# A mixture-of-experts stage on one core: expert weights split in halves ahead of their blocks, down projection in f16

## The chip, the core and the metric

The program runs on one core of one Trainium2 chip. Its time is the device time of one execution in microseconds (us). The core has TensorE (PE; its weight loads are listed apart as PEld), VectorE (DVE), ScalarE (ACT), GpSimd (POOL) and SyncE (SP), each with an instruction stream of its own; they meet at semaphores only. Transfers are issued from the queues of SP, ACT and POOL.

## What is computed

A block of an encoder on 4096 tokens of width 1024, in two stages. The mixer (norm, input projection, a linear recurrence beside a gated delta rule, output projection, residual) isn't changed in what it computes. Behind it each token goes to two of 32 experts, and each expert is a gated MLP with a hidden width of 256:

```
p_sel, g_sel = top_k(softmax(x @ group_w + group_b), 1)
top_logits, top_idx = top_k(expert logits of the chosen group, 2)
gates = p_sel * softmax(top_logits)
h = silu(xb @ w_gate[e]) * (xb @ w_up[e])      # 1024 -> 256
y = h @ w_down[e]                              # 256 -> 1024
out[token] += y * gate
```

A last norm follows. All inputs are f32. The 8192 assignments are sorted by expert; each expert's share is cut into blocks of 128 rows.

## The kernel before

**Mixer stage.** A software pipeline over 33 tiles of 128 tokens, written out by hand: `body(s)` of each engine names the parts of several tiles in one order. It takes 63 to 64 us a step and is followed by a table of the expert blocks (L1654 to L1684) that VectorE writes and TensorE turns into one row. Between other work, ScalarE also sums the squares of w_gate and w_up of one expert in each step from the fourth on (`raw_squares`, L917: eight chunks of 512 columns, squared in place in `ht`). SP loads the chunks into the two halves of `ht`, each when the square before the last is done (`raw_chunks`, L487). From the sums comes a scale for each expert, so that the weights fit f16. Step -1 has one expert to sum and step 0 has two; steps 1 and 2 have none.

**Expert stage.** `blocks` (L1810) runs 5 blocks written out, then pairs in a loop with a run-time limit, then two more. Each block knows its expert from a table `blk`. Four slots in `W` hold the raw f32 weights of four experts (1 MB each of gate, up and down); SP refills a slot when the last down product of its expert is done (L1854 to L1857), and says `w_ready` for the expert before. What one block asks of each engine, in program order:

- POOL gathers 128 rows of normed tokens (L1874), reads the next block's token numbers (L1866) and adds the output rows of three blocks earlier to `h_rows` in HBM (L1906).
- ScalarE makes the high f16 part of the next block's gate and up weights, eight instructions of 512 columns (`high_part`, L1982), each with a signal of its own; the sigmoid (L2002); the high part of the next rows (L1991); half of the previous block's output (L1968); the copy of the turned hidden rows, in f32 (L2009).
- VectorE makes the low part of the same weights, raw times scale minus high, eight instructions, each after its own high part (`low_part`, L2038); the hidden rows (L2061 and L2065, with the token's gate in the second); the low part of the next rows (L2022); the other half of the output (L2045); the column of scales for a later block (L2031).
- TensorE: gate/up in three f16 products (high x high, high x low, low x high; 24 matmuls of 512 columns, L1946), the turn of the next rows (L1920), the down product of the block before in f32 (four matmuls of 512 columns, shown as eight, L1930), the turn of the hidden rows (L1956).

The weights of an expert are thus split anew for each of its blocks, into two buffers `wx` in turn. A wait by VectorE in the low parts:

```
for k in range(KT):
    dve.wait_ge(sem("wx_high"), KT * b + k + 1)
    a = nc.vector.scalar_tensor_tensor(out=part_of(wx[par][:, 1], k), in0=raw[:, k], ...)
```

## Time and profile before

| | us |
|---|---|
| runs (three) | 3265.24, 3267.44 (median), 3268.61 |
| span of the profiled execution, first to last instruction | 3263.7 |
| PE busy | 2990.4 (92%) |
| DVE busy | 2590.6 (79%) |
| ACT busy | 1997.9 (61%) |
| POOL busy | 949.3 (29%) |

The time of the profiled execution itself isn't listed apart from these three; its span lies 3.7 us below their median, for what is around the first and last instruction. Busy time is time in which an engine executes; matmuls are pipelined, so that a duration of one is more than the distance to the next, and distances between starts are the ones to read. "[1.00 <-ACT W L1982]" behind a row means: the engine sat idle for 1.00 us until ScalarE's instruction of line 1982 on tile W was done; "issue" means that nothing the profile shows was waited for. The mixer stage fills the span up to about 2300 us, the expert stage up to about 3175, the last norm the rest. Mean granted TensorE clock: 0.968 of full speed.

### The profile page before, as it was taken

What the parts mean: (1) busy time and instruction counts of PE and PEld (TensorE: products, weight loads), DVE (VectorE), ACT (ScalarE), POOL (GpSimd) and SP (SyncE); (2) the same over time, 40 slices, a digit from 0 to 9 for tenths busy, and PEclk for the clock granted to TensorE, in tenths of its full rate; (3) what the DMA queues carried; (4) which work ended last, traced back from release to release, by engine and by line L of the source; (5) the groups of instructions that cost most, each with busy time, mean ns of one, the idle gap of its engine ahead of it and who ended that gap; (6) DMA issues with size and microseconds to landing.
All of it is one profiled execution on the core that took longest, in us unless ns stands there. A gap on an engine that the chain in (4) does not pass through costs nothing. (4 is left out here: it accounts for less than half of the span.)

```text
span 3263.7 us, 81939 instructions
## 1 busy us (share of the span) xinstructions
PE 2990.4 (92%) x28778; PEld 2233.3 (68%) x28779; DVE 2590.6 (79%) x7206; ACT 1997.9 (61%) x4412; POOL 949.3 (29%) x994
## 2 busy tenths in 40 slices
PE   3777999999999999999999999997699999999970
PEld 3766878888887888788878888885344555555430
DVE  6878778887887888788878887886788888888755
ACT  4555566666665656565666666653577777777646
POOL 4313122212221222132222212221344444544420
PEclk9889999999999999999999999998899999999985
DMA  7010111211212111212111111214387877677749
GB/s 264 27 53 14 47 66 65 67 66 66 72 63 76 60 67 66 73 60 73 66 66 65 68 66 66 72 56 200 118 255 222 243 202 214 187 219 216 220 99 394
DMA packets 117811, 380.30 MB, mean 117 GB/s; under 512 B 18560, under 2 KB 18688, under 8 KB 105216
## 3 DMA queue, kind: packets, MB, share of 16 engines
q1 hardware_dynamic: 82528, 269.96, 22.6%
q0 software_dynamic: 29216, 89.30, 11.9%
q10 hardware_dynamic: 5760, 16.85, 1.3%
q8 instruction: 204, 3.34, 0.4%
q14 instruction: 103, 0.84, 0.1%
HBM read 280.05 MB, written 96.01 MB: 115 GB/s over the span
## 5 line engine op out<-in xcount | busy, mean ns | idle before, releaser
L578 PE MATMUL pj<-uT,W 128*128 128x128 f16 x15840 | 982.9, 220 | 0.0
L578 PEld LDWEIGHTS pj<-uT,W 128*128 128x128 f16 x15840 | 936.8, 98 | 45.7 <-issue 37.6
L2038 DVE SCALAR_TENSOR_TENSOR W<-W,ecol 128x512 f16<-128x512 f16 x664 | 447.6, 747 | 111.9 <-ACT W L1982 107.4
L1982 ACT ACTIVATE W<-W,ecol 128x512 f16 x664 | 416.2, 710 | 79.7 <-issue 77.2
L1946 PE MATMUL bA<-W,uT 128*128 128x512 f16 x1992 | 446.6, 381 | 5.4 <-issue 4.1
L1946 PEld LDWEIGHTS bA<-W,uT 128*128 128x128 f16 x1992 | 193.5, 98 | 228.6 <-issue 9.1
L1741 POOL TENSOR_TENSOR dec<-tri,g 128x512 f32<-128x512 f32 x33 | 34.4, 1042 | 925.6 <-DVE g L1461 925.6
L1930 PE MATMUL pj<-W,qs 128*128 x664 | 301.8, 598 | 1.9 <-issue 1.0
L917 ACT ACTIVATE ht<-ht 128x512 f32<-128x512 f32 x256 | 159.9, 627 | 94.6 <-DMA ht<-w_up 90.2
L1930 PEld LDWEIGHTS pj<-W,qs 128*128 128x128 f32 x664 | 120.9, 192 | 123.3 <-issue 122.9
L947 ACT ACTIVATE qh<-bA 128x256 f32<-128x256 f32 x198 | 76.8, 388 | 193.4 <-PE bA L678 188.1
L638 PE MATMUL bO<-W,yl 128*128 128x512 f16 x768 | 186.4, 383 | 5.0 <-DVE yl L1375 5.0
L595 PE MATMUL pj<-W,uT 128*128 128x512 f16 x792 | 186.7, 379 | 0.5 <-POOL W L1692 0.5
L1777 POOL TENSOR_TENSOR yg<-aahh,gg 128x512 f32<-128x512 f32 x33 | 41.9, 1271 | 482.1 <-DVE yl L1375 457.8
L638 PE MATMUL bO<-W,yt 128*128 128x512 f16 x768 | 178.4, 378 | 0.0
L1155 DVE SCALAR_TENSOR_TENSOR qs<-ext_q,cvw,qs 128x128 f32<-128x128 f32 x396 | 168.2, 485 | 1.2
L678 PE MATMUL bA<-dec,Mt 128*128 128x128 f32 x792 | 134.2, 292 | 11.5 <-DVE dec L1303 11.1
L1906 POOL DMA_INDIRECT h_rows<-lath,sid x42 | 71.7, 1706 | 245.0 <-issue 121.1
L1906 POOL DMA_INDIRECT h_rows<-aahh,sid x41 | 71.0, 1731 | 203.6 <-issue 99.8
L595 PEld LDWEIGHTS pj<-W,uT 128*128 128x128 f16 x792 | 73.9, 98 | 71.7 <-issue 0.7
L1313 DVE COPY_PREDICATED X<-lvl,bB 128x256 f32<-128x256 uint8 x165 | 82.3, 499 | 50.5 <-PE bB L691 47.6
L691 PE MATMUL bB<-X,qh 128*128 128x128 f32 x660 | 113.4, 295 | 6.7 <-ACT qh L947 3.2
(444 smaller groups left out, 6310.0 us busy)
## 6 DMA issues: line engine op xcount, KB each, us to landing
ht<-w_gate SPq DMA_DIRECT2D x128, 256.0 KB, 3.2
ht<-w_up SPq DMA_DIRECT2D x128, 256.0 KB, 3.4
W<-w_gate SPq DMA_DIRECT2D x32, 1024.0 KB
W<-w_up SPq DMA_DIRECT2D x32, 1024.0 KB
W<-w_down SPq DMA_DIRECT2D x32, 1024.0 KB
x_in<-xm SPq DMA_DIRECT2D x33, 512.0 KB, 4.5
ht<-xm SPq DMA_DIRECT2D x32, 512.0 KB, 3.5
h_rows<-ht SPq DMA_DIRECT2D x32, 512.0 KB
```

The source lines that it names most:

```text
L578: mm = pe.matmul(pj[g % 2][:, j, :], w16[:, k, w_half(w_high, COL[GROUPS[g]], 512, j * P, P)], (ul if low_u else uh)[:, k, :], start=(k == ...
L595: mm = pe.matmul(flat(pj[1]), u[:, k, :], w16[:, k, w_half(w_high, c, 512)], start=(k == 0 and n_pass == 0), stop=(k == KT - 1 and n_pass ...
L638: mm = pe.matmul(bOf[:, 512 * half:512 * half + 512], y, wo16[:, j, w_half(w_high, 512 * half, 512)], start=(j == 0 and not w_high), stop= ...
L678: mm = pe.matmul(bA[:, q, :], Mt[:, 2 + q, :], crossed(T, b, P * q, HALF // b), start=True, stop=True)
L691: mm = pe.matmul(bB[:, q, :], Y[:, q, :], crossed(X, b, P * q, HALF // b), start=True, stop=True)
L917: nc.scalar.activation(ht[:, 512 * (c % 2):512 * (c % 2) + 512], ht[:, 512 * (c % 2):512 * (c % 2) + 512], ACT.Square, accum_out=sqc[:, n, ...
L1155: a = nc.vector.scalar_tensor_tensor(out=dst[:, j, :], in0=src, scalar=w, in1=dst[:, j, :], op0=ALU.mult, op1=ALU.add)
L1906: pool.indirect_dma_start(out=h_rows, out_offset=bass.IndirectOffsetOnAxis(ap=sid[par][:], axis=0), in_=yo[par], in_offset=None, compute_o ...
L1930: mm = pe.matmul(flat(pj[half]), hm2[:, j, :], w[:, j, 512 * half:512 * half + 512], start=(j == 0), stop=(j == 1))
L1946: mm = pe.matmul(flat(bA), x[:, k, :], wx[par][:, part, k, :], start=(k == 0 and part == 0 and x is uh), stop=(k == KT - 1 and x is ul))
L1982: nc.scalar.activation(part_of(wx[par][:, 0], k), raw[:, k], ACT.Copy, scale=ecol[par][:, k:k + 1]).then_inc(sem("wx_high"), 1)
L2038: a = nc.vector.scalar_tensor_tensor(out=part_of(wx[par][:, 1], k), in0=raw[:, k], scalar=ecol[par][:, k:k + 1], in1=part_of(wx[par][:, 0] ...
```

## The change

- **Splitting.** Each expert now has two halves (four of the eight gate/up pieces, and one of the two rows of w_down each). In every block ScalarE makes four high parts and VectorE four low ones of a half of the *next* expert, in a buffer per parity of the expert: block 0 of an expert the first half, every later block the second. VectorE waits once, for all four high parts. The first expert is split whole ahead of block 0. Each expert gets at least two blocks (`LEAST`), so that both halves are made.
- **Down projection.** w_down is split also, with a scale of its own (1024 columns in each half, one instruction on each engine). The hidden rows are divided by their largest absolute value, turned, and split into high and low f16; three f16 products take the place of the f32 one (12 matmuls of 512 columns). The row's scale and gate go into the evacuation, all of which is now ScalarE's.
- **Raw slots.** Three instead of four. SP refills a slot when its expert is split, and says `w_ready` for an expert in its next iteration.
- **Sums of squares.** Twelve chunks instead of eight for each expert in the mixer stage; the four of w_down are squared at other places of `body`.
- The table has more columns (expert ahead, addresses of raw and split weights), read by six small matmuls instead of three.

The diff, cut to its core:

```diff
-ZEROED = 16 * (IDX_FILLS + 2)
-WSLOTS = 4
+ZEROED = 16 * (IDX_FILLS + 3)
+RAW_SLOTS = 3
+SQ = SLOT // 512
+LEAST = 2
+HM_TOP = 16384.0
 # ScalarE, mixer stage
-                                raw_squares(s, 2 * g - 2, 2 * g - 1)
-                        raw_squares(s, 6, 7)
+                                raw_squares(s, 3 * g - 3, 3 * g - 2, 3 * g - 1)
+                        raw_squares(s, 9, 10, 11)
                     level_y(s, 5)
                     if s.G:
+                        raw_squares(s, 2)
                         need(act, sem("y_lru"), s.nG)
...
+                    if s.G:
+                        raw_squares(s, 3)
                     level_y(s, 6)
...
-                        raw_squares(s, 2, 3)
+                        raw_squares(s, 4, 5)
...
-                        raw_squares(s, 4, 5, 6)
+                        raw_squares(s, 6, 7, 8)
...
-                        raw_squares(s, 7)
+                        raw_squares(s, 9, 10)
                     if s.P:
                         need(act, sem("conv"), 16 * s.nP)
                         nc.scalar.activation(vs[:], vs[:], ACT.Silu).then_inc(sem("qkv_silu"), 1)
+                    if s.G:
+                        raw_squares(s, 11)
                     if s.P:
                         nc.scalar.preload_act_table_set("natural_log_exp_and_others")
 # the table
+                table_link(nc.vector.tensor_scalar(nb, nb, float(LEAST), None, ALU.max))
 # SP, expert stage
+                for e in range(RAW_SLOTS, NE):
+                    sp.wait_ge(sem(f"w_loaded{e % RAW_SLOTS}"), 48 * (e // RAW_SLOTS))
+                    sp.sem_inc(sem("w_ready"), 2)
+                    split = sp.value_load(starti[0:1, e - RAW_SLOTS:e - RAW_SLOTS + 1], min_val=2, max_val=NITER)
+                    sp.wait_ge(sem("wd_low"), split)
+                    settle(sp)
+                    load_expert(sp, e, e % RAW_SLOTS)
 # TensorE
                 def down(b):
-                    w = W[:, bass.ds(slot_of(pe, b) + GU, WD)].rearrange("p (j n) -> p j n", j=2)
-                    pe.wait_ge(sem("hm2_ready"), b + 1)
...
+                    w = weights(b)
+                    pe.wait_ge(sem("hm_low"), b + 1)
+                    pe.wait_ge(sem("wd_low"), b + 2)
+                    need(pe, sem("yo_ready"), b)
                     for half in range(2):
-                        for j in range(2):
-                            mm = pe.matmul(flat(pj[half]), hm2[:, j, :], w[:, j, 512 * half:512 * half + 512],
-                                           start=(j == 0), stop=(j == 1))
+                        for part, h in ((1, 0), (0, 0), (0, 1)):
+                            for j in range(2):
+                                a = 2 * GU + 2 * UNIT * j + D * part + 512 * half
+                                mm = pe.matmul(flat(pj[half]), hm16[:, h, j, :], w[:, a:a + 512],
+                                               start=(j == 0 and part == 1), stop=(j == 1 and h == 1))
 # ScalarE, expert stage
                     if not last:
-                        high_part(b + 1, 1 - par)
+                        loaded = act.value_load(blk2[0:1, bass.ds(3 * b, 1)], min_val=3, max_val=2 * NE)
+                        raw, split = raw_unit(act, b), split_unit(act, b)
+                        act.wait_ge(sem("w_ready"), loaded)
+                        act.wait_ge(sem("ecol_ready"), b + 1)
+                        need(act, sem("gu_full"), b)
+                        gu_high(raw, split, lambda half, k: ecol[par][:, k:k + 1], range(1))
                     act.wait_ge(sem("gu_full"), b + 1)
...
-                    nc.scalar.activation(sm, flat(bA)[:, 0:FE], ACT.Sigmoid, scale=ecol[par][:, KT:KT + 1]).then_inc(sem("silu_sig"), 1)
+                    nc.scalar.activation(sm, flat(bA)[:, 0:FE], ACT.Silu, scale=ecol[par][:, 5:6]).then_inc(sem("silu"), 1)
                     if not last:
                         x_part(b + 1)
                     if not (isinstance(b, int) and b == 0):
-                        out_half(b - 1, 1 - par)
+                        out_rows(b - 1, 1 - par)
                     act.wait_ge(sem("hm_turned"), b + 1)
                     need(act, sem("y_full"), b + 1)
-                    nc.scalar.activation(hm2, bT[:, 0:2, :], ACT.Copy).then_inc(sem("hm2_ready"), 1)
+                    nc.scalar.activation(hm16[:, 0], bT[:, 0:2, :], ACT.Copy).then_inc(sem("hm_high"), 1)
+                    if not last:
+                        act.wait_ge(sem("y_full"), b + 1)
+                        down_high(raw, split, ecol[par][:, 4:5], range(1))
 # VectorE, expert stage
+                def gu_low(raw, split, cols, halves):
+                    for half in halves:
+                        for k in range(4):
+                            a = nc.vector.scalar_tensor_tensor(out=split_gu(split, half, 1, k), in0=raw_gu(raw, half, k),
+                                                               scalar=cols(half, k), in1=split_gu(split, half, 0, k),
+                                                               op0=ALU.mult, op1=ALU.subtract)
+                        a.then_inc(sem("wx_low"), 1)
+                def hidden(b, par):
+                    def step(ins, k):
+                        ins.then_inc(sem("hm_step"), 1)
+                        dve.wait_ge(sem("hm_step"), 4 * b + k)
...
+                    step(nc.vector.tensor_copy(gcol[par][:], gall[:, bass.ds(b, 1), 1:2].bitcast(F32).rearrange("p a c -> p (a c)")), 1)
+                    nc.vector.tensor_tensor(gcol[par][:], gcol[par][:], ecol[par][:, 6:7], ALU.mult)
+                    dve.wait_ge(sem("silu"), b + 1)
+                    need(dve, sem("hm_turned"), b)
+                    ins = nc.vector.tensor_tensor(hm, sm, flat(bA)[:, FE:2 * FE], ALU.mult)
+                    ins.then_inc(sem("gu_used"), 1)
+                    dve.wait_ge(sem("gu_used"), b + 1)
+                    step(nc.vector.tensor_reduce(hcol[par][:, 0:1], hm, AX, ALU.max, apply_absolute_value=True), 2)
+                    step(nc.vector.tensor_scalar(hcol[par][:, 0:1], hcol[par][:, 0:1], 1e-30, None, ALU.max), 3)
+                    nc.vector.tensor_tensor(hcol[par][:, 1:2], hcol[par][:, 0:1], gcol[par][:], ALU.mult).then_inc(sem("oc_ready"), 1)
+                    step(nc.vector.reciprocal(hrec[:], hcol[par][:, 0:1]), 4)
+                    nc.vector.tensor_scalar(hm, hm, hrec[:], HM_TOP, ALU.mult, ALU.mult).then_inc(sem("hm_ready"), 1)
 # VectorE's block
                     if not last:
+                        raw, split = raw_unit(dve, b), split_unit(dve, b)
+                        dve.wait_ge(sem("wx_high"), b + 3)
+                        gu_low(raw, split, lambda half, k: ecol[par][:, k:k + 1], range(1))
+                    hidden(b, par)
+                    if not last:
                         turned(b + 1)
+                    dve.wait_ge(sem("hm_high"), b + 1)
+                    nc.vector.tensor_tensor(hm16[:, 1], bT[:, 0:2, :], hm16[:, 0], ALU.subtract).then_inc(sem("hm_low"), 1)
+                    if not last:
+                        dve.wait_ge(sem("wd_high"), b + 3)
+                        down_low(raw, split, ecol[par][:, 4:5], range(1))
+                        dve.wait_ge(sem("wd_low"), b + 3)
                         columns(b + 2, par)
```

## Rows read from the trace of the kernel before

**Rows 1.** Page, busy us of the engines, and the costliest lines (busy, mean ns of one).
```profile
PE 2990.4 (92%) x28778; PEld 2233.3 (68%) x28779; DVE 2590.6 (79%) x7206; ACT 1997.9 (61%) x4412; POOL 949.3 (29%) x994
...
L1946 PE MATMUL bA<-W,uT 128*128 128x512 f16 x1992 | 446.6, 381 | 5.4 <-issue 4.1
```

**Rows 2.** Windows: width, PE, PEld, DVE, ACT, POOL busy us (count); granted clock, DMA share, GB/s.
```profile
143.00:206.00 63.00, 51.48 (x658) 46.17 (x658) 45.02 (x115) 34.89 (x80) 14.03 (x13) 0.95 0.17 60
...
2720.00:2820.00 100.00, 100.00 (x427) 51.70 (x426) 84.86 (x165) 72.91 (x132) 46.19 (x50) 1.00 0.73 205
```

**Rows 3.** Timeline of one expert block: start us, us, engine, line, operation, count [idle before].
```profile
2800.63 5.34 PE L1946 MATMUL bA<-W,uT 128*128 128x512 f16 x24
...
2801.18 0.38 ACT L2009 ACTIVATE qs<-bT 128x256 f32<-128x256 f32 x1
...
2802.29 5.01 ACT L1982 ACTIVATE W<-W,ecol 128x512 f16 x8 [0.74 <-issue]
...
2803.16 5.39 DVE L2038 SCALAR_TENSOR_TENSOR W<-W,ecol 128x512 f16<-128x512 f16 x8 [1.00 <-ACT W L1982]
...
2805.81 1.06 PE L1920 MATMUL bO<-ident,ht 128*128 128x128 f32 x8
...
2806.70 3.60 PE L1930 MATMUL pj<-W,qs 128*128 x8
...
2808.47 0.41 DVE L2061 TENSOR_TENSOR xc<-xc,bA 128x256 f32<-128x256 f32 x1
...
2809.01 0.48 DVE L2065 SCALAR_TENSOR_TENSOR xc<-xc,gcol,bA 128x256 f32<-128x256 f32 x1
...
2810.14 0.39 PE L1956 MATMUL bT<-ident,xc 128*128 128x128 f32 x2
...
2810.43 0.60 ACT L1968 ACTIVATE aahh<-pj 128x512 f32<-128x512 f32 x1 [1.80 <-PE pj L1930]
...
2810.46 5.34 PE L1946 MATMUL bA<-W,uT 128*128 128x512 f16 x24
```

**Rows 4.** Timeline: TensorE's first and last gate/up product.
```profile
2319.75 6.82 PE L1946 MATMUL bA<-W,uT 128*128 128x512 f16 x24 [1.18 <-ACT uT L1991]
...
3149.51 5.34 PE L1946 MATMUL bA<-W,uT 128*128 128x512 f16 x24
```

**Rows 5.** Groups by line: 1024 wide operations of VectorE and ScalarE.
```profile
L2134 DVE SCALAR_TENSOR_TENSOR W<-W,aahh 128x1024 f32<-128x1024 f32 x32 | 41.1, 1285 | 55.5 <-ACT aahh L2116 55.5
...
L2112 ACT ACTIVATE junk<-W 128x1024 bf16<-128x1024 f32 x32 | 33.8, 1057 | 28.2 <-DMA W<-h_rows 27.7 <-issue 0.5
```

**Rows 6.** Timeline: VectorE's 512 wide scaling, and two linked small operations.
```profile
1520.21 0.43 DVE L1480 TENSOR_SCALAR dec<-dec 128x512 f32<-128x512 f32 x1
...
2302.12 0.16 DVE L1671 TENSOR_TENSOR tcol<-iota_p,tcol 128x1 f32<-128x1 f32 x1
2302.32 0.15 DVE L1672 TENSOR_SCALAR tcol<-tcol 128x1 f32<-128x1 f32 x1
```

**Rows 7.** Timeline: TensorE's turn of the hidden rows, SP's first and third load.
```profile
2829.70 0.39 PE L1956 MATMUL bT<-ident,xc 128*128 128x128 f32 x2
...
2830.10 0.34 SPq L421 DMA_DIRECT2D W<-w_gate  x1
...
2831.01 0.38 SPq L421 DMA_DIRECT2D W<-w_down  x1
```

**Rows 8.** Timeline of a step of the mixer stage.
```profile
1566.29 0.63 ACT L917 ACTIVATE ht<-ht 128x512 f32<-128x512 f32 x1 [2.57 <-DMA ht<-w_up]
...
1550.12 0.39 ACT L947 ACTIVATE qh<-bA 128x256 f32<-128x256 f32 x1
...
1551.26 0.66 PE L691 MATMUL bB<-X,qh 128*128 128x128 f32 x4
...
1524.28 0.68 DVE L1497 TENSOR_TENSOR Mt<-bA,decb 128x512 f32<-128x512 f32 x1
...
1525.37 0.38 PE L748 MATMUL bT<-ident,Mt 128*128 128x128 f32 x2
```

More of the change, by code:

```diff
@@ L48 @@
 SLOT = GU + WD
+UNIT = 1024
+SQ = SLOT // 512
+HALF_ROW = 7
+NITER = P
+LEAST = 2
+HM_TOP = 16384.0
 RSTEPS = 19
@@ L1659, in _ @@
                 table_link(nc.vector.tensor_tensor(start, end, nb, ALU.subtract))
-                nc.vector.tensor_scalar(endi, end, 1.0, None, ALU.add)
+                nc.vector.tensor_scalar(starti, start, 2.0, None, ALU.add)
                 nc.vector.tensor_scalar(blk[:, 3 * P:3 * P + 1], end[0:1, NE - 1:NE], 0.5, -1.25 - FEWEST, ALU.mult, ALU.add
                                         )
+                expert, pos, half, odd, third = (tcol[:, n:n + 1] for n in (0, 1, 8, 9, 10))
+                row, pe_off, idx_off, next_row, raw_off, split_off = (tcol[:, n:n + 1] for n in range(2, 8))
@@ L2069, in body @@
                         columns(b + 2, par)
-                    if not (isinstance(b, int) and b == 0):
-                        out_half(b - 1, 1 - par)
-                    if last:
-                        out_half(b, par)
                 blocks(dve, body)
```

291 lines of the change are left out of this document (161 added, 130 removed).

## The prediction

> **What bounds the kernel now.** I read the table of costly lines first, then busy times by stretch, then one block of the expert stage in order of time. The gate/up matmuls number 1,992, 24 a block, so 83 blocks run [rows 1]; TensorE is busy for 92% of the span. In a stretch of 100 us of expert blocks TensorE shows 100.00 us busy, VectorE 84.86, ScalarE 72.91 [rows 2]. The block shows why [rows 3]: gate/up issues for 5.18 us (2800.63 to 2805.81), the eight turns of the next rows 0.89, the f32 down product 3.44, the two turns of the hidden rows 0.32; the next gate/up follows at once. That is 9.83 us. From the first gate/up to the last, 82 periods take 3149.51 - 2319.75 = 829.8 us [rows 4], 10.12 each: 0.29 more, in waits outside this block. TensorE is the bound, but hardly: ScalarE's eight copies begin at 2802.29 and last 5.01, VectorE's eight low parts follow each by 0.87, then two products of 0.54 and 0.48; the hidden rows are ready at 2809.49, only 0.65 before TensorE turns them at 2810.14.
>
> **Number of blocks.** Routing the reference's seeded inputs gives 32 expert counts whose sum of ceil(count/128) is 82, run as 83. Three experts hold 128 or fewer (60, 75, 92), so at least two blocks each makes 85. The periods become 84.
>
> **TensorE per block.** The down product becomes 12 f16 matmuls 512 wide instead of four f32. 24 such ones take 5.18 us, 0.216 each, so 12 take 2.59: 0.85 saved. TensorE alone needs 5.18 + 0.89 + 2.59 + 0.32 = 8.98 us.
>
> **The ring through ScalarE and VectorE.** This I take as the new bound. Before, each low part followed its own high part; now VectorE waits for the last of four high parts, and only then makes four low parts, and only behind these the hidden rows. Clock it from the start of the turn of the hidden rows, time 0:
> - the turn reaches ScalarE at 0.32 + 0.29 = 0.61 (0.29 is from the end of the down product's issue, 2810.14, to ScalarE's 2810.43 [rows 3]); the high hidden part takes 0.38: 0.99. Evacuation of the previous output (now both halves on ScalarE, about 1.05) runs before it, in the time that TensorE now idles.
> - the high down part, 1024 wide, 1.06 [rows 5]: 2.05. Three registers must be read for the next block. With two, 1.11 us passed from the start of the short copy to the start of the next high part (2801.18 to 2802.29) [rows 3]; for three I take 1.66 from 0.99: high parts start at 2.65.
> - four high parts, half of 5.01: 5.15; VectorE starts about 0.15 later, 5.3. Its own work (low hidden part, low down part, columns, four register reads) ends at 3.45 and then about 2 us of reads, so 5.4: a near tie.
> - four low parts, half of 5.39, 2.70: 8.05.
> - the gate column, copy and product, 0.36; the product silu times up 0.54 [rows 3]; the maximum over 256, not in the trace, between one small operation (0.2) and 256 wide product (0.54), I take 0.45, nearer the latter since it reads as many; clamp, scale, reciprocal at a pitch of 0.20 for two that wait for each other and less for one that doesn't [rows 6], 0.55; scaling of 256 columns, between 0.15 for one column and 0.43 for 512 [rows 6], 0.30. Together 2.20: 10.25, and TensorE 0.1 later: **10.4 us** a block.
> The silu itself is hidden: gate/up ends at 5.5 and ScalarE is free at 5.2. Lower bound: register reads vanish below the down part and the small operations cost 1.7: 9.3. Upper bound: reads as long as 2.2 on ScalarE or VectorE not free before 6.0, and 2.8 of small operations: 11.5. All of it lies above 8.98, so I count none of TensorE's 0.85.
>
> **The loads in the ring.** SP now makes expert k+1 known as ready only in the iteration after the one that waits for the low down part of the block before expert k begins and issues three loads. That low part ends at 2.15 + 1.29 [rows 5] = 3.45. SP's first load starts 0.40 after the turn, thus 0.1 after the down product is done, and the third one 0.91 later and lasts 0.38 [rows 7]: 1.4 us of queue. ScalarE gets the sign at 5.0, not 2.65, although the bytes have long landed. So the block in which an expert begins takes 2.35 more: about 12.7. It holds for 28 periods (the first expert's gate lies at the start, the last three have none).
> Blocks: 28 x 12.7 + 56 x 10.4 = 355.6 + 582.4 = 938.0 us, against 829.8: **+108**. The traffic stays the same but for two more blocks; rows are gathered 12 us ahead instead of 10, so I count nothing for DMA, at most 10. If its cover went, TensorE would wait for rows within the 1.4 us that it idles now.
>
> **Start and end of the stage.** The first expert is split whole before anything else: VectorE's low parts start after all eight high parts and are followed by two down parts. The first gate/up starts as before, since its rows come late, but its last third waits until about 2323.6: +3 (0 to 7). The table takes six small matmuls more and unlinked column operations: +3 (1 to 5). The shorter down product at the end: -1.5.
>
> **The mixer stage.** Squares of w_down add four of 0.63 (with 0.19 for the sum, overlapped) to each of 29 steps, on ScalarE, with two buffers of chunks in turn. Where three follow each other one waits 2.57 us for its chunk already [rows 8], and still does, in the same place: no change. Two new ones hurt. Two squares ahead of the sixth level's copy push it from 1550.12 to about 1551.4; TensorE takes the result at 1551.26, 0.76 after it was there [rows 8]: some 0.5 us. One before the table load moves ScalarE by 0.62 and with it VectorE's product at 1524.28, 0.68 long, which TensorE turns at 1525.37, a slack of 0.41 [rows 8]: 0.25. 29 x 0.75 = 22, between 0 (slack is more than it looks) and 29 x 1.9 = 55 (nothing hides). The two steps at the beginning have one round trip and eight squares more: +11 (0 to 25). Together **+33**.
>
> **Sum.** 108 + 3 + 3 - 1.5 + 33 = +146 on the span of 3263.7: 3409. The median of the runs, 3267.4, lies 3.7 above this span; with that, about **3412 us**, 4.4% slower.
>
> **Rivals.**
> 1. TensorE stays the bound, faster. It decides if the ring closes in under 8.98. Then 84 x (8.98 + 0.29) = 779, -51, and with the smallest of the other costs about +15: 3231. For it: fewer ScalarE and VectorE instructions in each block (four high parts, not eight). Against: they no longer overlap, and even my lower bound is 9.3. 0.08.
> 2. SP's sign is not late (the change of expert costs nothing): 84 x 10.4 = 874, +44, with the others +81: 3348. For it: the loads are long landed; against: the order of SP's program. 0.14.
> 3. The ring is longer, at 11.2 and 13.5: 56 x 11.2 + 28 x 13.5 = 1005, +175, with the others: 3480. 0.15.
> 4. TensorE's clock falls to its lower level in the gaps of 12.7 - 8.98 = 3.7 us. Rows: the stretch 143 to 206 has TensorE busy for 51.48 of 63 us with a granted clock of 0.95, against 1.00 in full blocks [rows 2]; the first gate/up, after 11 us of idleness, took 6.82 instead of 5.34 [rows 4]. At 1.5 us for each of 28 gaps, 42: 3454. 0.13. The Trainium skill, "TensorE: Matmul & The Clock Gate", section "HAM oscillation", says that idle gaps between groups of matmuls throttle the array anew each time; by that rule every first block of an expert would pay, by the rows it is open, since none shows such gaps in a rhythm.
> 5. The change doesn't do what it says: the split "once per expert" goes on in each block, third blocks repeating the second half. I hold that for certain and it is in the sum; it makes no case of its own.
> My forecast has 0.46; 0.04 is left for costs that cancel.
>
> **Numbers.** Cases on the slow side reach from 3335 (rival 2 with a smaller mixer cost) to 3490 (rival 3), and leave out the faster case and the far ends. A measurement of this kernel can tell 0.2% from no change. Faster by over that 0.09, within it 0.03, slower 0.88.
>
> **What would show it.** Gate/up starts 10.4 apart within an expert and 12.7 where one begins; TensorE waiting for the product of VectorE at the hidden turn, 1.4 us a block; ScalarE's first high part waiting for SP at each new expert; 1,992 matmuls become 85 x 24 = 2,040; the first gate/up about 36 us later than 2319.75. I am wrong if TensorE shows no idle time in blocks, if steps of the mixer stay at their length, or if the VectorE chain after the last low part is much shorter than 2.2 us.

## Result and the profile after

The changed kernel takes 3635.9 us (median of 4 runs, 3633.0 to 3639.8) against 3268.0 for the kernel before beside it: 1.1122 times as long, 95% interval 1.1109 to 1.1135. The profiled run spans 3638.2 us, 374.5 more than before. The forecast was +146 on the span: the direction is right, the size is short by 228 us.

The page of the changed kernel: busy time of each engine, then the costliest lines of the expert stage and of the squares (busy, mean ns | idle time ahead of them).

```profile
PE 3070.6 (84%) x29208; PEld 2257.7 (62%) x29209; DVE 2563.8 (70%) x7466; ACT 2037.5 (56%) x4529; POOL 907.1 (25%) x1005
...
L2016 PE MATMUL bA<-W,uT 128*128 x2040 | 549.6, 435 | 99.5 <-issue 97.7
...
L2123 DVE SCALAR_TENSOR_TENSOR W<-W,ecol x336 | 230.1, 747 | 183.8 <-ACT W L2049 92.0
L930 ACT ACTIVATE ht<-ht 128x512 f32<-128x512 f32 x384 | 239.7, 627 | 148.8 <-DMA ht<-w_down 95.2
L2049 ACT ACTIVATE W<-W,ecol x336 | 214.7, 714 | 157.7 <-SPq L1912 88.7
...
L2026 PE MATMUL bT<-ident,xc 128*128 128x128 f32 x170 | 41.4, 328 | 194.2 <-DVE xc L2154 189.2
...
L2116 DVE COPY ecol<-zs 128x5 f32 x86 | 14.8, 172 | 186.3 <-issue 186.3
```

No engine is the bound any more: TensorE fell from 92% busy to 84% although it does more blocks [rows 1]. The last two lines lead to the cause. TensorE stands 194 us in front of the hidden rows' turn (L2026), and VectorE stands 186 us in front of a copy of five columns that takes 0.17 us. "issue" means that the profile shows nothing that it waited for: the engine's own sequencer is at work, here with register reads (shown below). The gate/up matmuls are 2,040 = 85 x 24, as forecast, and one lasts 435 ns on average instead of 381 [rows 1].

A window of the expert stage (TensorE, weight loads, VectorE, ScalarE, GpSimd; granted clock, DMA share, GB/s) answers to the last row of [rows 2]: in 100 us TensorE is busy 76, VectorE 56, and the granted clock is 0.88 instead of 1.00.

```profile
2500.00:3000.00 500.00, 378.81 (x1697) 187.74 (x1695) 279.01 (x654) 246.00 (x407) 137.74 (x185) 0.88 0.57 159
```

**Where the 374.5 us are.** The table load that ends the last mixer step is at 2264.98 instead of 2218.43: +46.6. The first turn of hidden rows is at 2379.67 instead of 2328.17, so the table and the start give +4.9. The last is at 3533.16 instead of 3158.13: 84 periods take 1153.5 us where 82 took 830.0, +323.5. From the last turn to the end: 105.0 instead of 105.5, -0.5.

The periods come in pairs, a half of mostly 13.5 us behind the turn of an even block and one of mostly 13.8 behind that of an odd block (means 13.50 and 13.82; from the fifth period to the end of the loop all lie between 13.0 and 14.2), whether an expert begins or not. The timeline of the changed kernel over one such pair (start, us, engine, line, operation, [idle before]), which answers to [rows 3]:

```profile
2908.49 0.39 PE L2026 MATMUL bT<-ident,xc 128*128 128x128 f32 x2
...
2908.72 5.34 PE L2016 MATMUL bA<-W,uT 128*128 x24
2908.78 1.26 ACT L2041 ACTIVATE lath<-pj,hcol 128x512 f32<-128x512 f32 x2 [1.59 <-PE pj L1998]
2909.93 0.38 ACT L2091 ACTIVATE qs<-bT 128x256 f16<-128x256 f32 x1
2910.19 1.16 ACT L2056 ACTIVATE W<-W,ecol  x1
...
2911.23 2.56 ACT L2049 ACTIVATE W<-W,ecol  x4
2911.65 1.28 DVE L2131 SCALAR_TENSOR_TENSOR W<-W,ecol  x1 [0.88 <-ACT W L2056]
...
2915.64 0.17 DVE L2116 COPY ecol<-zs 128x5 f32 x1 [2.71 <-issue]
2915.80 0.17 DVE L2117 COPY ecol<-zs 128x2 f32 x1
...
2917.58 2.74 DVE L2123 SCALAR_TENSOR_TENSOR W<-W,ecol  x4 [1.61 <-issue]
...
2920.50 0.42 DVE L2147 TENSOR_TENSOR xc<-xc,bA 128x256 f32<-128x256 f32 x1
...
2921.87 0.35 DVE L2154 TENSOR_SCALAR xc<-xc,wm 128x256 f32<-128x256 f32 x1
...
2922.28 0.61 PE L2026 MATMUL bT<-ident,xc 128*128 128x128 f32 x2 [4.73 <-DVE xc L2154]
...
2924.99 7.50 PE L2016 MATMUL bA<-W,uT 128*128 x24 [2.10 <-issue]
...
2927.62 2.56 ACT L2049 ACTIVATE W<-W,ecol  x4 [3.28 <-SPq L1912]
...
2932.32 1.05 PE L1980 MATMUL bO<-ident,x_in 128*128 128x128 f32 x8
...
2933.21 2.75 PE L1998 MATMUL pj<-W,qs 128*128 x12
...
2934.72 0.35 DVE L2154 TENSOR_SCALAR xc<-xc,wm 128x256 f32<-128x256 f32 x1
...
2935.80 0.39 PE L2026 MATMUL bT<-ident,xc 128*128 128x128 f32 x2
```

Half one, 2908.49 to 2922.28, is VectorE's. ScalarE's high parts are all there at 2913.79, but VectorE begins its low parts only at 2917.58: between its low part of w_down (done at 2912.93) and them lie 2.71 and 1.61 us with nothing on the engine, around two small copies. The records of VectorE's sequencer show what fills them: four register reads, each a TENSOR_LOAD with its register arithmetic. Three take 0.7 to 0.8 us each, 0.30 to 0.39 of it the load. The second one (L2114, the table number for the expert ahead) has a load of 1.31 us; 13 us later, in half two, the same line takes 0.30:

```profile
L2114 DVEq TENSOR_LOAD <-ext_q x2: 302/808/1315, 2913.8 to 2926.7; - x2
```

(Shortest, median and longest of two, in ns.) In all 39 odd blocks of the loop this load took 1.16 to 1.39 us, and each time GpSimd was at the gather of the next rows (L1935) and the instructions behind it; in the even blocks, with nothing of GpSimd beside it in 35 of 40, it took 0.30 to 0.31. That is a coincidence in time, and no run tests it. Half two, 2922.28 to 2935.80, is TensorE's: 2.71 us to the start of gate/up, 2.10 of them "issue"; gate/up takes 7.33 instead of 5.18, since the granted clock has fallen after 4.73 us of idleness (its mean over the window above is 0.88); then 0.89 and 2.59. These add up to 13.52, the whole half. The 2.71 us hold the end of the loop's pass (0.65) and one register read, whose load alone takes 1.17. VectorE's hidden rows are done at 2935.07, 0.7 us earlier, so another chain is close behind.

### The profile page after: what moved, and what is told of

It is laid out like the page before. It is cut to its first block and busy times, and to the rows that moved or that the text cites. A ratio compares the mean times of both kernels' runs of the same rounds, so it can differ in the third digit from the quotient of the medians.

```text
span 3638.2 us, 86111 instructions
## 1 busy us (share of the span) xinstructions
PE 3070.6 (84%) x29208; PEld 2257.7 (62%) x29209; DVE 2563.8 (70%) x7466; ACT 2037.5 (56%) x4529; POOL 907.1 (25%) x1005
## 3 DMA queue, kind: packets, MB, share of 16 engines
q0 software_dynamic: 29888, 91.40, 11.4%
## 5 line engine op out<-in xcount | busy, mean ns | idle before, releaser
L2016 PE MATMUL bA<-W,uT 128*128 x2040 | 549.6, 435 | 99.5 <-issue 97.7
L2016 PEld LDWEIGHTS bA<-W,uT 128*128 128x128 f16 x2040 | 223.1, 109 | 401.2 <-issue 234.2
L2123 DVE SCALAR_TENSOR_TENSOR W<-W,ecol x336 | 230.1, 747 | 183.8 <-ACT W L2049 92.0
L930 ACT ACTIVATE ht<-ht 128x512 f32<-128x512 f32 x384 | 239.7, 627 | 148.8 <-DMA ht<-w_down 95.2
L2049 ACT ACTIVATE W<-W,ecol x336 | 214.7, 714 | 157.7 <-SPq L1912 88.7
L1998 PE MATMUL pj<-W,qs 128*128 x1020 | 234.0, 379 | 1.0 <-DVE qs L2174 1.0
L2026 PE MATMUL bT<-ident,xc 128*128 128x128 f32 x170 | 41.4, 328 | 194.2 <-DVE xc L2154 189.2
L2026 PEld LDWEIGHTS bT<-ident,xc 128*128 128x128 f32 x170 | 29.9, 201 | 221.2 <-DVE xc L2154 210.1
L1998 PEld LDWEIGHTS pj<-W,qs 128*128 128x128 f16 x1020 | 100.1, 98 | 102.6 <-issue 1.2
L2131 DVE SCALAR_TENSOR_TENSOR W<-W,ecol x84 | 108.0, 1286 | 71.6 <-ACT W L2056 71.6
L2116 DVE COPY ecol<-zs 128x5 f32 x86 | 14.8, 172 | 186.3 <-issue 186.3
L691 PE MATMUL bA<-dec,Mt 128*128 128x128 f32 x792 | 134.7, 293 | 10.7 <-DVE dec L1321 10.5
```

Source lines behind the costliest of these rows:

```text
L691: mm = pe.matmul(bA[:, q, :], Mt[:, 2 + q, :], crossed(T, b, P * q, HALF // b), start=True, stop=True)
L930: nc.scalar.activation(ht[:, 512 * (c % 2):512 * (c % 2) + 512], ht[:, 512 * (c % 2):512 * (c % 2) + 512], ACT.Square, accum_out=sqc[:, n, ...
L1998: mm = pe.matmul(flat(pj[half]), hm16[:, h, j, :], w[:, a:a + 512], start=(j == 0 and part == 1), stop=(j == 1 and h == 1))
L2016: mm = pe.matmul(flat(bA), x[:, k, :], w[:, a:a + 512], start=(k == 0 and part == 0 and x is uh), stop=(k == KT - 1 and x is ul))
L2049: a = nc.scalar.activation(split_gu(split, half, 0, k), raw_gu(raw, half, k), ACT.Copy, scale=cols(half, k))
L2123: a = nc.vector.scalar_tensor_tensor(out=split_gu(split, half, 1, k), in0=raw_gu(raw, half, k), scalar=cols(half, k), in1=split_gu(split, ...
```

## The experiments

"Against" in the results means the changed kernel's 3636 us, unless another is named. The kernel before, run beside each group of them, took 3263.5 to 3267.6 us. Periods are counted between the starts of the turns of the hidden rows.

### One part at a time

**VectorE's column copy ahead of the hidden rows.**

```diff
     gu_low(raw, split, lambda half, k: ecol[par][:, k:k + 1], range(1))
+    if not (isinstance(b, int) and b == 0):
+        dve.wait_ge(sem("wd_low"), b + 2)
+        columns(b + 1, 1 - par)
     hidden(b, par)
...
     down_low(raw, split, ecol[par][:, 4:5], range(1))
-    dve.wait_ge(sem("wd_low"), b + 3)
-    columns(b + 2, par)
```

> Edit: VectorE reads its two table registers and copies the next block's column right behind the low parts of gate and up, ahead of the hidden rows, so the reads no longer stand between the low part of w_down and the signal that ScalarE and VectorE's next low parts go by. Theory A (the register reads of VectorE close the ring: 4.3 us of idle VectorE in the slow half of a pair, of which only the part behind the wait for the low part of w_down can leave): a pair of blocks falls from 27.3 us to 22 to 24.6 us, 42 pairs give 110 to 220 us, so 3415 to 3525 us. Theory B (SyncE's signals, or ScalarE's output rows, set the slow half and the reads only fill the wait for them): within 20 us of 3636 us. Theory C (the reads cost the same wherever they stand, the chain is VectorE's own): within 20 us of 3636 us too, with the idle time now shown ahead of the hidden rows.

3539.7 us: -96, theory A's direction, somewhat less than its lower figure. Theories B and C fall. The mean period is 12.53 instead of 13.73. Two consecutive blocks of this run:

```profile
2808.63 0.50 PE L2026 MATMUL bT<-ident,xc 128*128 128x128 f32 x2 [0.52 <-DVE xc L2154]
...
2819.83 0.50 PE L2026 MATMUL bT<-ident,xc 128*128 128x128 f32 x2 [0.51 <-DVE xc L2154]
...
2822.56 2.56 ACT L2049 ACTIVATE W<-W,ecol  x4 [0.55 <-issue]
...
2825.39 2.74 DVE L2123 SCALAR_TENSOR_TENSOR W<-W,ecol  x4 [1.79 <-ACT W L2049]
...
2828.04 0.17 DVE L2116 COPY ecol<-zs 128x5 f32 x1
```

The reads have gone from the front of the copy (2828.04 has no idle time before it), and VectorE now waits for ScalarE. From the turn at 2819.83 the high parts begin at 2.73 and the low parts at 5.56; and the period from there is 10.44 us, the shortest of the run but for the last, and found again and again. That is the ring which the prediction had drawn: 2.65, 5.4, 10.4. Other periods, up to 14.8, remain.

**SyncE's signal before its wait for the slot.** The signal for an expert is given as soon as its load has landed.

```diff
+    for e in range(RAW_SLOTS - 1):
+        sp.wait_ge(sem(f"w_loaded{e}"), 48)
+        sp.sem_inc(sem("w_ready"), 2)
     for e in range(RAW_SLOTS, NE):
-        sp.wait_ge(sem(f"w_loaded{e % RAW_SLOTS}"), 48 * (e // RAW_SLOTS))
+        sp.wait_ge(sem(f"w_loaded{(e - 1) % RAW_SLOTS}"), 48 * ((e - 1) // RAW_SLOTS + 1))
         sp.sem_inc(sem("w_ready"), 2)
...
```

> Edit: SyncE's signal for an expert is given when its load has landed, before the wait that its slot asks for, so it is never late for the half that begins an expert. Theory of the prediction (the late signal lengthens 28 expert-first blocks by 2.35 us): minus 66 us, 3570 us. Theory A (the wait of 3.28 us for SyncE falls into the half of the pair that has time to spare, since slow and fast halves alternate whether an expert begins or not): no more than 10 us, 3626 to 3640 us, and the idle time of ScalarE behind SyncE (88.7 us) becomes idle time behind something else.

3631.6 us: -4. The wait on SyncE disappears from the high parts altogether. Their idle time falls from 157.7 us, 88.7 of them SyncE's, to 92.8, and all that is left is "issue":

```profile
L2051 ACT ACTIVATE W<-W,ecol x336 | 214.7, 715 | 92.8 <-issue 92.8
```

The signal was late as predicted (5.34 us behind the turn, forecast 5.0) but worth next to nothing here. In the changed kernel ScalarE waited for it 26 times. 17 of these lie in halves like half two, where TensorE ends last anyhow. The other 9 lie in halves like half one, where the high parts were done at 8.3 to 9.2 us behind the turn and VectorE's reads hold its low parts until 9.1 (2917.58 - 2908.49) anyhow.

**Both of these.** No new edit.

> Edit: the column ahead of the hidden rows (as in the run that gave 3540 us) and SyncE's early signal (3632 us by itself) together. Theory A (with the reads out, the shortest ring is the 10.44 us seen in that run, and the blocks at 13 to 14.5 us are those in which ScalarE waits for SyncE's signal; the signal was hidden before only because the reads were longer): the long blocks fall to 11 us, mean block 11.0 to 11.4 instead of 12.5, minus 95 to 125 us against 3540, so 3415 to 3445 us. Theory B (the weights land late, the signal is right): within 20 us of 3540 us.

3439.5 us, -100 against the 3539.7 of the first alone, with a mean period of 11.40. So the same edit is worth 4 us or 100, depending on what stands beside it. The late signal had been covered, by VectorE's reads in one half and by TensorE in the other. It costs more than the 66 us of the prediction once it is bare.

**The loop's bound.**

```diff
...
-    with eng.Fori(2, (NITER - 4) // 2) as p:
+    with eng.Fori(2, 46) as p:
```

> Edit: the upper bound of the run-time loop is 46 pairs again, as before the change, instead of 62 (this input needs 42). Theory A (each empty pair that the loop still runs through after the last block costs 0.7 to 0.8 us, 16 pairs fewer): minus 12 us, 3624 us, and the last block's gate and up start 5 us behind the last hidden turn instead of 17. Theory B (the 12 us at the end are the wait for the last scattered rows): no change, 3636 us.

3627.7 us: -8. The last blocks show it directly; first the changed kernel, where TensorE has been idle since the last block of the loop (the period is 27.66 us), then this run:

```profile
3512.94 7.08 PE L2016 MATMUL bA<-W,uT 128*128 x24 [16.68 <-issue]
```

```profile
3499.73 7.92 PE L2016 MATMUL bA<-W,uT 128*128 x24 [4.68 <-issue]
```

16 fewer empty passes took 12.0 us off TensorE's idle time, 0.75 each; the period is 16.52 instead of 27.66. Theory A, with 8 of its 12 us found in the times, and 12.5 between the spans of the two profiled runs. The records of TensorE's sequencer show what such a pass is: two compare-and-branch instructions of 0.22 us each and two register operations, with short gaps between them.

**The squares of w_down left out.** Everywhere as in this line, and ScalarE's squares stand at the places that they had before the change; the scale of w_down is taken from the sums of gate and up; the rest is as in the change.

```diff
-    for c in range(SQ):
+    for c in range(KT):
```

> Edit: the squares of w_down are left out: 8 chunks for each expert as before the change, at the old places of ScalarE's program, and the scale of w_down is taken from the sums of gate and up. Theory A (the four more chunks for each expert, with their loads, are the whole loss of the mixer stage): the table is loaded at 2218 us again instead of 2265, minus 47 us, 3589 us. Theory of the prediction: minus 33 us, 3603 us. Theory B (the loss comes from the other edits: the wider table, its start, the placement of loads): less than 15 us.

3597.8 us: -38, between theory A (-47) and the prediction's 33. The last table load is at 2225.67 (below) instead of 2264.98, so 39 of the 46.6 us are the squares; 7 are not, and no run took them apart. The place of this load differs by several us between runs here that have the same mixer stage (2260.60 in the kernel of 3349 us, 2266.26 in that of 3581), so both figures are rough.

```profile
2225.67 1.28 ACT L1130 ACT_TABLE_LOAD   x1
```

**TensorE's read moved.** It reads the next block's address while it waits for the hidden rows, and keeps it in a register for the gate/up matmuls.

```diff
+    if not last:
+        pe.reg_load(wreg, blk[0:1, bass.ds(3 * (b + 1) + 1, 1)])
     pe.wait_ge(sem("hm_ready"), b + 1)
```

> Edit: TensorE reads the address of the next block's weights while it waits for the hidden rows, instead of at the head of the next block; VectorE and ScalarE keep their reads. Theory A (TensorE's reads, 2.1 to 2.7 us between a hidden turn and the gate and up matmuls in one half of each pair, lie in the path): minus 2 us in 42 pairs, 3550 us. Theory B (the half in which gate and up start late by that is the half in which VectorE's low parts of the next block are late anyway, so the read is beside the ring): within 25 us of 3636 us.

3581.1 us: -55, between the theories and nearer to A. Turn to gate/up falls from 2.7 to 1.0 us in half two, but that half gets only 0.7 shorter on average (12.77 for 13.50): there VectorE's chain, which was 0.7 us behind, now ends last. The rest comes from half one, shorter by as much (13.07 for 13.82). The down product is now done before VectorE has the hidden rows, so ScalarE begins the output rows ahead of the turn instead of behind it, and copies the turned rows 0.83 us after the turn instead of 1.44:

```profile
2909.53 1.26 ACT L2047 ACTIVATE lath<-pj,hcol 128x512 f32<-128x512 f32 x2 [1.59 <-PE pj L1998]
...
2909.85 0.51 PE L2032 MATMUL bT<-ident,xc 128*128 128x128 f32 x2 [0.44 <-DVE xc L2160]
...
2910.68 0.38 ACT L2097 ACTIVATE qs<-bT 128x256 f16<-128x256 f32 x1
```

**A filler for the clock.**

```diff
+    if par == 0 and not last:
+        for n in range(14):
+            pe.matmul(bC[:, 0, :], ident[:], ident[:], start=True, stop=True)
     pe.wait_ge(sem("hm_ready"), b + 1)
```

> Edit: 14 matmuls of 128 columns in f32 on the identity, into a bank that nothing reads, before TensorE's wait for the hidden rows of every even block, where it stands idle for 4.7 us. They last about 3.5 us. Theory A (the shortfall of the granted clock, 0.87 instead of 1.00, stretches gate and up from 5.2 to 7.3 us in one half of each pair and so lengthens the path): the clock of the expert stage rises to 0.95 or more, gate and up take 5.2 to 5.8 us in both halves, up to 2.1 us less in each of 42 pairs: 3550 to 3600 us. Theory B (the ring runs through ScalarE and VectorE, and TensorE's slow stretch lies beside it): the clock rises and the time stays within 15 us of 3636 us.

3632.7 us, no difference; granted clock 0.92 in the window from 2500 to 3000. That looks like theory B, but the timeline forbids a clean verdict. In the filled half the filler itself holds up the turn, and the long wait has moved to the other half, where gate/up is still slow:

```profile
2906.52 0.50 PE L2029 MATMUL bT<-ident,xc 128*128 128x128 f32 x2 [3.67 <-DVE xc L2157]
...
2907.62 7.04 PE L2016 MATMUL bA<-W,uT 128*128 x24 [0.59 <-issue]
...
2917.97 3.29 PE L2025 MATMUL bC<-ident 128*128 128x128 f32 x28
...
2921.33 5.34 PE L2016 MATMUL bA<-W,uT 128*128 x24
```

In the half behind the filler gate/up starts at once and runs at the full clock (5.18 us), and that half gets only 0.9 us shorter (12.56 on average for 13.50), because VectorE ends last there, 3.5 us behind TensorE. The other half gets 0.9 longer.

### What a register read costs

**Two reads more, first attempt.**

```diff
+    for c in range(2):
+        dve.reg_load(spare, blk[0:1, bass.ds(3 * b + 1 + c, 1)])
     settle(dve)
```

> Edit: the kernel after the change with two register reads more on VectorE, beside the two that stand ahead of its column copies behind the low part of w_down; what they read is not used. Theory A (a register read behind a wait costs VectorE 0.8 us each, and in one half of a pair it lies in the path; in the other there is slack for it): the idle time ahead of the column copy grows by 1.6 us, and the pair by 1.6 us: plus 67 us, 3700 us; at most 3.2 us a pair, 3770 us. Theory B (the reads are hidden behind other engines' work): within 15 us of 3636 us.

3639.1 us, and 2.69 us ahead of the copy as before. Nothing used what was read, and the profile counts 86,111 instructions, exactly as many as for the changed kernel (the next run has 860 more): the reads weren't in the program that ran. The run says nothing about either theory.

**Two reads more that are used.**

```diff
-    nc.vector.tensor_copy(ecol[par][:, 0:5].unsqueeze(1), half_rows[:, bass.ds(ahead, 1), 0:5])
+    for c in range(2):
+        again = dve.value_load(blk2[0:1, bass.ds(3 * b, 1)], min_val=3, max_val=2 * NE)
+        nc.vector.tensor_copy(ecol[par][:, 2 * c:2 * c + 2].unsqueeze(1), half_rows[:, bass.ds(again, 1), 2 * c:2 * c + 2])
+    nc.vector.tensor_copy(ecol[par][:, 4:5].unsqueeze(1), half_rows[:, bass.ds(ahead, 1), 4:5])
```

> Edit: the kernel after the change; VectorE's copy of five columns is cut into three copies, and two of these read the table number again by themselves, so that the two reads more are used and stay in the program (those of the run that gave 3639 us were used by nothing, and its trace shows the same 2.69 us ahead of the copy, so they were dropped). Theory A (a read behind a wait costs VectorE 0.8 us, and lies in the ring in one half of each pair): 2 reads and 0.25 us of copies more, 1.9 us a pair, plus 80 us, 3716 us; at most in both halves, plus 160 us. Theory B (reads are hidden, and the gain of the kernel with the column ahead of the hidden rows came from the order of the work alone): within 20 us of 3636 us.

3703.1 us: +67, theory A. The place of the added reads:

```profile
2915.34 0.17 DVE L2118 COPY ecol<-zs 128x2 f32 x1 [3.29 <-issue]
...
2916.12 0.17 DVE L2118 COPY ecol<-zs 128x2 f32 x1 [0.60 <-issue]
2916.27 0.15 DVE L2119 COPY ecol<-zs 128x1 f32 x1
2916.41 0.17 DVE L2120 COPY ecol<-zs 128x2 f32 x1
```

The idle time ahead of the first copy grew from 2.71 to 3.29, and 0.60 stands between two copies: about 0.6 us for a read that nothing covers, 0.30 of it the load itself. From the end of the low part of w_down to the last of these copies the path grew by 1.5 us. The pair grew by 1.64 (mean period 14.55 against 13.73), 1.0 in half one and 0.6 in half two; 42 pairs give 69.

### Putting it together

**All edits, and a signal for each of the four high parts,** so that a low part follows its own high part as it did before the change.

```diff
-    a = nc.scalar.activation(split_gu(split, half, 0, k), raw_gu(raw, half, k), ACT.Copy,
-                             scale=cols(half, k))
-    a.then_inc(sem("wx_high"), 1)
+    nc.scalar.activation(split_gu(split, half, 0, k), raw_gu(raw, half, k), ACT.Copy,
+                         scale=cols(half, k)).then_inc(sem("wx_high"), 1)
...
+    dve.wait_ge(sem("wx_high"), seen + k + 1)
```

> Edit: all of these together (column ahead of the hidden rows, SyncE's early signal, the loop's bound of 46, TensorE's read moved) and a signal for each of ScalarE's four high parts, so that VectorE's low parts follow one part behind instead of behind all four. Theory A (the ring of 10.44 us loses 2.0 us by the following; then TensorE, alone 8.98 us a block, is the bound and the clock is full): 9.0 to 9.6 us a block, 84 blocks 756 to 806 us instead of 1153, with 8 us for the loop: 3225 to 3285 us. Theory B (register reads of VectorE and TensorE remain in the ring, which only shifts): 10.4 us a block, 3365 us.

3349.5 us: -286 against the changed kernel, still 2.7% above the kernel before. Mean period 10.31: theory B's number. The granted clock is 1.00 again. The ring had not gone:

```profile
2909.24 2.56 ACT L2057 ACTIVATE W<-W,ecol  x4 [1.29 <-issue]
...
2910.89 2.74 DVE L2132 SCALAR_TENSOR_TENSOR W<-W,ecol  x4 [1.36 <-ACT W L2057]
```

ScalarE stands idle for 1.29 us ahead of its high parts (0.58 in the other half), VectorE for 1.36 ahead of its low parts (0.53): the reads of the addresses of raw and split weights, which all lie between the down parts and the gate/up parts.

**The same without the squares of w_down.**

> Edit: the kernel that gave 3349 us, with the squares of w_down left out (its scale is taken from the sums of gate and up). Expected: the 38 us that this gave by itself, as the mixer stage and the expert stage share no work: 3311 us. If the expert stage starts earlier and its first loads are late, less than 30 us.

3314.7 us, -35: the mixer's price adds up by itself, as expected.

**ScalarE's and VectorE's address reads a block ahead.** ScalarE reads after the copies of x, VectorE after the low parts of x, into registers kept for each parity.

```diff
     x_part(b + 1)
+    read_ahead(act, aregs[1 - par], b + 1, 0)
```

> Edit: the same, and ScalarE and VectorE read the addresses of the next block's raw and split weights one block ahead into registers kept for it, ScalarE while it waits for the down projection, VectorE while it turns the rows. Theory A (in the kernel of 3349 us 1.3 and 0.6 us of ScalarE's reads and 1.4 and 0.5 us of VectorE's stood in the ring; without them TensorE's own sum of 9.1 and 9.8 us a block is the bound): mean block 9.45 instead of 10.31 us, minus 72 us: 3235 to 3255 us, faster than before the change. Theory B (the reads cost the same wherever they stand): 3311 us, as the run without them moved.

3306.4 us: only -8, where 72 were expected. The high parts now follow at once, the low parts too, but in the half shown the copy of the columns has 0.97 us of idle time before it, and TensorE waits 1.50 us for the hidden rows: the other two reads of VectorE are the next in the ring.

```profile
2906.72 0.17 DVE L2137 COPY ecol<-zs 128x5 f32 x1 [0.97 <-issue]
...
2909.22 0.50 PE L2041 MATMUL bT<-ident,xc 128*128 128x128 f32 x2 [1.50 <-DVE xc L2177]
```

**Those two as well, the filler (5 matmuls), and both.** One column read goes behind the low part of the hidden rows, the other behind the low part of w_down.

```diff
+    dve.reg_load(cregs[0], blk[0:1, bass.ds(3 * (b + 2), 1)])
     dve.wait_ge(sem("wd_high"), b + 3)
     down_low(raw, split, ecol[par][:, 4:5], range(1))
+    dve.reg_load(cregs[1], blk2[0:1, bass.ds(3 * (b + 2), 1)])
```

> Edit: the kernel that gave 3306 us, with the two table numbers of the column copies read ahead too, one behind the low part of the hidden rows, one behind the low part of w_down. Theory A (that kernel gained 8 us where 72 were expected because its column reads, 0.97 us ahead of the copy in one half of each pair, came to stand in the ring; TensorE then idles 1.5 us and its clock falls, gate and up last 6.9 instead of 5.2 us): the pair falls from 20.3 us to 18.9 to 19.5 us, minus 33 to 58 us, 3250 to 3273 us. Theory B (the other reads, moved ahead, have made the ring longer elsewhere): 3306 us or more.

> Edit: the kernel that gave 3306 us, with 5 matmuls of 128 columns in f32 (1.2 us) on the identity, ahead of TensorE's wait for the hidden rows of each even block, where it stands idle for 1.5 us. Theory A (here, unlike in the kernel after the change, TensorE is the bound of the half that follows, so the clock that falls in the gap costs 1.5 us a pair): clock of the expert stage 1.00 throughout, gate and up 5.2 to 5.4 us in both halves, minus 50 to 63 us: 3243 to 3256 us. Theory B (the granted clock is not what stretches the half): within 10 us of 3306 us.

> Edit: both of the last two together. If the column reads and the clock are one cause (the reads make the gap, the gap costs the clock), the second edit adds nothing to the first: 3245 to 3275 us, within 10 us of the better of the two. If they are two, it is faster than either by 15 us or more.

With the column reads moved: 3257.4 us, -49, theory A. Against the kernel before 0.9972, 95% interval 0.9959 to 0.9985: 0.3% faster. The filler alone: 3297.7 us, -9; it removed the six periods of 11.2 to 11.4 us, in which gate/up had taken 6.7 to 6.9 us instead of 5.2, and left the usual pair of 9.7 and 10.5; 6 x 1.5 is the 9 us. In the other 33 even halves of the loop gate/up ran at full speed although TensorE had idled about 1.5 us ahead of nearly all of them too. Theory B, then, in this kernel: reads, not the clock, held the pair. Both: 3252.7 us (0.9947, 0.9929 to 0.9965), 5 us below the better one. The runs of the two overlap (3246.9 to 3261.1 and 3252.2 to 3267.9), so this is one cause, and whether anything remains beside it is not shown. The kernel with the column reads moved, in order of time:

```profile
2903.08 0.16 DVE L2146 COPY ecol<-zs 128x5 f32 x1
...
2905.26 0.51 PE L2041 MATMUL bT<-ident,xc 128*128 128x128 f32 x2
...
2906.30 5.35 PE L2029 MATMUL bA<-W,uT 128*128 x24 [0.54 <-issue]
...
2909.50 2.74 DVE L2155 SCALAR_TENSOR_TENSOR W<-W,ecol  x4
...
2914.97 0.39 PE L2041 MATMUL bT<-ident,xc 128*128 128x128 f32 x2
...
2915.20 5.34 PE L2029 MATMUL bA<-W,uT 128*128 x24
```

TensorE is nearly the bound again: periods of 9.18 and 9.72, TensorE busy for 96% of the window from 2500 to 3000 (its own sum is 8.98, and up to 1.0 lies between turn and gate/up in one half). This version leaves out the squares of w_down; with them it would be some 35 us slower, an estimate from the two runs that differ in that alone, and so slower than the kernel before.

## Why the prediction was wrong

- **Number of blocks, TensorE per block, hidden chain: right.** 85 blocks; 12 down matmuls issue in 2.59 us (2933.21 to 2935.80); gate column to scaled rows 1.98 us for 2.20.
- **The ring as the new bound: right, and 10.4 us is its length** where none of VectorE's reads ends last (10.44).
- **The step that failed: "Its own work (low hidden part, low down part, columns, four register reads) ends at 3.45 and then about 2 us of reads, so 5.4: a near tie."** The term for the reads was sized at less than half. Low parts start at 2917.58 - 2908.49 = 9.09. The low part of w_down ended at 4.44 instead of 3.45 (the output rows, 1.26 us on ScalarE, held up the high hidden part until 1.44, where the prediction had put them into idle time). From there to the low parts it was 4.65 instead of about 1.95. The prediction had the order right: the reads stand behind the wait for the low part of w_down, so none begins under it. It priced each at about 0.5 us, after ScalarE's two in the block of [rows 3]. VectorE's took 0.7 to 0.8 us three times and 1.7 once, with the long load of 1.31; that is 3.8 of the 4.65, and the rest is the addressing of the copies and of the low parts. The run with two used reads more gives 0.6 us for one more. Why one load of four takes 1.0 us longer, in every odd block, stays open.
- **TensorE's own read was not counted at all:** 2.10 us of "issue" ahead of gate/up in one half of each pair, worth 55 us by the run that moved it, half of that through ScalarE's output rows. The code shows it: `weights(b)` at the head of each block, where the kernel before used its buffers without a read (the read in the down product was there before).
- **SyncE's signal (2.35 us in 28 blocks, 66 us): the signal was late, but worth 4 us here.** Rival 2, that the change of expert costs nothing, came out, though not for its reason (that the loads are long landed): the sign was late 26 times, and each time something else was as late or later, TensorE in half two and VectorE's reads in half one. With the column reads out of the way it was worth 100.
- **The clock (rival 4): mechanism right, price small.** The waits of 4.7 us were followed by gate/up at about 7.4 instead of 5.2 us, in 42 halves and not 28. The Trainium skill, "TensorE: Matmul & The Clock Gate", section "HAM oscillation", describes a kernel whose waits between groups of matmuls throttled the array anew each time; the trace agrees with that for these waits, while after the waits of 1.5 us in the kernel of 3306 us gate/up was slow in only 6 of 39 halves. TensorE ended last in that half by only 0.7 us, so a full clock could shorten the half itself by about 0.7 x 42 = 30 us, and as much again might come from half one, as it did when TensorE's read was moved; these are estimates, and no run here measured the clock alone.
- **Empty passes of the loop: not foreseen,** 8 us in the times. Its bound rose from 46 to 62 with the change.
- **The mixer: +33 forecast, +46.6 measured,** inside its bounds; 39 of it are the squares. A steady step grew by 65.35 - 64.42 = 0.93 us (table loads at 1545.40 and 1610.75; before at 1559.53 and 1623.95) where 0.75 was forecast, and the start with the first step by 5.8 + 9.1 = 14.9 against 11. The chunk wait ahead of squares rose from 94.6 to 148.8 us in all, 95.2 of them for w_down. The first gate/up comes at 2368.43, 48.7 us later than before where 36 was forecast.
- **From span to time:** in every run here the time is 1.6 us above the span. The 3.7 us that the prediction added hold 2 us of scatter between runs; it doesn't matter for a miss of 224.
- **Rival 1 fell:** TensorE is not the bound of the changed kernel. In the last kernels the ring closes in little more than TensorE's sum of 8.98 (periods from 9.18), and there its shorter down product does count.
- **Rival 3, a longer ring, points the right way but not far enough:** it had 11.2 and 13.5 us, 3480 in all; every block took 13.5 or more on average, with or without a new expert.

In one sum: 28 x 12.7 + 56 x 10.4 were 938 us; measured were 1153.5, of which 12 are empty passes. The remaining 203 are 42 pairs at about 4.9 us. Half one is 3.4 longer than the ring's 10.4 (0.99 late, 2.70 reads, 0.3 less behind them). Half two is 3.1 longer by TensorE's read and clock, and 1.6 of that stood in the sum already, under SyncE's name.

## What to carry to other kernels

Count every register read that a dynamic address needs, on each engine, and ask what it stands behind: a read under queued work cost nothing here (TensorE's in half one, under the down product), one more behind a semaphore wait 0.6 to 0.7 us on VectorE, and up to 1.7 in the worst place. Eight of them moved, with SyncE's signal given early, the shorter loop and finer signals, took the expert stage from 13.7 to 9.7 us a block; the part of each is not additive. Price edits in combination, since a late signal was worth 4 us with the reads in place and 100 without them. And when a loop with a run-time end gets a larger bound, each pass that it skips has to be paid as well.

## What the runs showed of the hardware that was not expected

- A register read whose value is used took VectorE about 0.6 us of "issue" (0.60 idle between two copies that otherwise follow at once); an unused one was not in the program that ran.
- The load inside such a read took 0.30 us on VectorE at its shortest, but 1.16 to 1.39 in one place of every odd block, and 1.18 (median of 39) in TensorE's read at the head of the loop's pass. The long ones on VectorE coincide with GpSimd's gather of the next rows. This is why 2.71 us stand ahead of the column copy in half one and 1.62 ahead of the same copy, with the same two reads, in half two; what makes the load long stays open.
- A loop pass with nothing in it took 0.75 us (12.0 us for 16). The Trainium skill, "Advanced Engine Details and Errata", section "Control Flow Timing", gives about 108 ns for a compare-and-branch; the trace differs, with 0.22 us for each of the two in a skipped pass on TensorE, and the rest of the 0.75 is two register operations and what lies between.
- After the edits four periods early in the stage, at 13.9 to 16.0 us, remain in the kernel of 3257 us. In each of them TensorE waits 3.1 to 3.8 us for the gathered rows of the next block (`ht<-u_rows,gid`), a transfer that the slower ring had covered: the changed kernel has no such wait of over 1 us behind the first block.
